# Three blocks of a transformer on one core: the rounded parts of the weights in a ring of four, split in the middle of a chunk

## What is computed

```
def _attention_layer(...):
    h = _rmsnorm(x, pre_g) * (1 + scale) + shift
    proj = h @ w_in                       # q, k, v, z
    outA = _dense_attention(...); outB = _window_attention(...)
    y = jnp.concatenate([outA, outB], axis=-1) * jax.nn.silu(z)
    x = x + gate * _rmsnorm(y @ w_out, post_g)

def _pool_layer(...):
    proj = h @ w_in
    y = _multiscale_pool(...) * jax.nn.silu(proj[..., POOL_WIDTH:])
    x = x + gate * _rmsnorm(y @ w_out, post_g)

def second_block(...):
    proj = h @ w_in[layer]
    q_sb, k_sb, v_sb, z_sb, q_r, k_r, v_r, z_r = jnp.split(proj, split_at, axis=-1)
    oa = stick_breaking_attention(...) * silu(z_sb)
    qr = rotary(q_r); kr = rotary(k_r) * HEAD_DIM ** -0.5
    ob = head_group_norm(chunkwise_retention(qr, kr, vr), gain) * silu(z_r)
    x = x + gate * (jnp.concatenate([oa, ob], axis=-1) @ w_out[layer])
```

## Time and profile before

| | us |
|---|---|
| median of three runs | 2598.04 |
| the three runs | 2602.52, 2598.04, 2596.53 |
| the profiled execution | 2595.46 |
| its span | 2593.6 |

### The profile page before, as it was taken

How to read it: one execution, slowest core, us unless ns; L and a number is a source line. 1 busy time by engine, 2 the same in 40 slices (tenths; PEclk the granted TensorE clock), 3 DMA queues, 4 the chain that set the end, 5 groups by cost and what they waited for, 6 DMA issues and landing times.

```text
span 2593.6 us, 29840 instructions
## 1 busy us (share of the span) xinstructions
PE 2528.2 (97%) x11859; PEld 2027.7 (78%) x11859; DVE 1617.3 (62%) x2424; ACT 958.3 (37%) x1529; POOL 105.1 (4%) x115
## 2 busy tenths in 40 slices
PE   7999999999999999999999998999999999999998
PEld 4789777777777877888888887887788777787786
DVE  4456666677776758677776757356466477656432
ACT  4222434434454333332334333355455423233321
POOL 0000000000000103000000102000000000000000
PEclk8999999999999989999999998999999999999999
DMA  9945433444425745666645654323222255532342
GB/s 349 340 163 187 125 111 114 122 124 133 133 90 169 241 150 171 195 203 207 207 146 194 239 176 141 93 79 90 74 87 83 77 164 160 172 93 82 122 146 73
DMA packets 292877, 390.58 MB, mean 151 GB/s; under 512 B 11698, under 2 KB 221234, under 8 KB 288898
## 3 DMA queue, kind: packets, MB, share of 16 engines
q1 hardware_dynamic: 286608, 354.79, 43.0%
q0 software_dynamic: 6128, 33.89, 3.4%
q10 hardware_dynamic: 2, 0.00, 0.0%
HBM read 371.85 MB, written 16.78 MB: 150 GB/s over the span
## 4 chain that ended last, share of the span: by engine, by line
PE 91%; DVE 4%; DMA 2%; ACT 1%; issue 1%; SPq 1%; POOL 0%; ACTq 0%; POOLq 0%; DVEq 0%
PE G L1962 77%; PE S L1962 6%; PE OB L1962 5%; PE TB L1965 2%; PE TB L1962 1%; DMA MORE<-in_ev_mod_w 1%; DMA MRAW<-in_ev_mod_w 1%; DVE Y L1473 1%; DVE TT L1473 1%; SPq L1019 0%; PE OB L1965 0%; DVE WLO L1473 0%; DMA LATE<-in_ev_mod_w 0%; DVE HLO L1479 0%; DVE SQ L1479 0%
## 5 line engine op out<-in xcount | busy, mean ns | idle before, releaser
L1962 PE MATMUL G<-HHI,WHI 128*128 128x512 f32 x2624 | 1088.9, 415 | 28.5 <-issue 7.7
L1962 PE MATMUL G<-HHI,WLO 128*128 128x512 f32 x2624 | 1031.2, 393 | 0.0
L1962 PE MATMUL G<-HLO,WHI 128*128 128x512 f32 x2624 | 1028.3, 392 | 0.0
L1473 DVE TENSOR_TENSOR WLO<-RAW,WHI 128x1024 fp32r<-128x1024 f32 x376 | 459.2, 1222 | 282.5 <-ACT WHI L1139 279.4
L1139 ACT ACTIVATE WHI<-RAW 128x1024 fp32r<-128x1024 f32 x376 | 394.8, 1054 | 583.1 <-PE G L1962 543.7
L1962 PEld LDWEIGHTS G<-HHI,WHI 128*128 128x128 f32 x2624 | 497.2, 189 | 139.2 <-issue 23.5
L1962 PEld LDWEIGHTS G<-HHI,WLO 128*128 128x128 f32 x2624 | 495.9, 189 | 108.4
L1962 PEld LDWEIGHTS G<-HLO,WHI 128*128 128x128 f32 x2624 | 498.0, 190 | 104.8 <-issue 8.1
L1479 DVE SCALAR_TENSOR_TENSOR MACC<-MWIDE,SC,MACC 128x512 f32<-128x512 f32 x420 | 321.3, 765 | 39.5 <-DMA MWIDE<-in_od_mod_w 13.5
L1962 PE MATMUL G<-WHI,HHI 128*128 128x512 f32 (+1 forms) x384 | 145.0, 378 | 3.9 <-ACT K L1139 3.0
L1962 PE MATMUL G<-WLO,HHI 128*128 128x512 f32 (+1 forms) x384 | 136.4, 355 | 0.0
(11 more groups left out here) (274 smaller groups left out, 2346.8 us busy)
## 6 DMA issues: line engine op xcount, KB each, us to landing
RAW<-in_w_in SPq DMA_DIRECT2D x128, 512.0 KB, 3.7
MWIDE<-in_od_mod_w SPq DMA_DIRECT2D x96, 512.0 KB, 4.2
MWIDE<-in_w_ada SPq DMA_DIRECT2D x96, 512.0 KB, 4.5
RAW<-in_ev_w_in SPq DMA_DIRECT2D x80, 512.0 KB, 3.8
RAW<-in_od_w_in SPq DMA_DIRECT2D x64, 512.0 KB, 3.9
MWIDE<-in_ev_mod_w SPq DMA_DIRECT2D x32, 512.0 KB, 3.9
RAW<-in_ev_w_out SPq DMA_DIRECT2D x32, 512.0 KB, 3.6
RAW<-in_od_w_out SPq DMA_DIRECT2D x32, 512.0 KB, 3.5
```

Source lines behind the costliest of these rows:

```text
L1473: return e.o.tensor_tensor(o, a, b, op)
L1962: return e.o.matmul(o, l, r, start=start, stop=stop, skip_group_check=True)
```

## The change

`NS` becomes 4. The ring WHI gets a fourth place, for the chunks with i % 4 = 3; the three others keep their tiles. The fourth lies over TA[0] and TA[1] (`WHI_TA`) as long as no stick-breaking head runs, and over Y[14] and Y[15] (`WHI_Y`) from chunk 232 to 299, while they do. Where a place changes its owner there are added waits: ACT's cast of the first chunk in Y waits for the spill of layer 3's input and its last tile, that of the next chunk in TA for the last stick-breaking sums, the first use of TA for chunk 231 (`last_ta`), and the last two rows of Y in layer 3 for chunk 299 (`last_y`).

The split moves from the end of a chunk to its middle (`split_ahead`), in `gemm_dual` behind the first pair of a chunk's matmul groups, ahead of `next(tiles)`. There it is that of chunk i + 3.

```
-    NR, NS = 5, 3
+    NR, NS = 5, 4
...
-    WHI = [place(f"WHI{i}", [P, 4, 256], F32R)[0] for i in range(NS)]
+    WHI3 = [place(f"WHI{i}", [P, 4, 256], F32R)[0] for i in range(3)]
...
+    WHI_TA = scratch("WHITA", [P, 4, 256], F32R, 46 * K1)
+    WHI_Y, _ = place("WHIY", [P, 4, 256], F32R, y0 + 4 * SEQ * 14)
...
+    stick0, stick1 = first_chunk[third + 2], first_chunk[third + 16] + 4
+    fourths = range(3, len(chunks), 4)
+    last_ta = max(i for i in fourths if i < stick0)
+    first_y = min(i for i in fourths if i >= stick0)
+    last_y = max(i for i in fourths if i < stick1)
+    next_ta = min(i for i in fourths if i >= stick1)
+
+    def whi(i):
+
+        if i % 4 < 3:
+            return WHI3[i % 4]
+        return WHI_Y if stick0 <= i < stick1 else WHI_TA
...
+        def split_ahead(i):
+            while at["split"] < min(i + NS, len(chunks)):
+                split_next()
...
@@ unit
-                while at["split"] < min(i + NS, len(chunks)):
-                    split_next()
...
@@ gemm (gemm_two, gemm_tok and gemm_wide alike)
                         put("mm", kind, layer, u, i, c, nt, jj, pair, last)
+                        if nt == 0 and jj:
+                            split_ahead(i)
                         step(background)
...
@@ gemm_dual
                     for nt in range(2):
                         put("mm2", "h", layer, u, i, c % 2, c // 2 * 4, nt, jj, (first + c) % 2)
+                    if jj == 0:
+                        split_ahead(i)
                     next(tiles, None)
                 used(i)
-                while at["split"] < min(i + NS, len(chunks)):
-                    split_next()
...
@@ act_program, stage "split"
+                if i == first_y:
+                    e.wait_ge(spill, 3)
+                    e.wait_ge(v_tile, (3, KT - 1))
+                elif i == next_ta:
+                    e.wait_ge(p_cum, (7, 0))
+                    e.wait_ge(v_st, (7, 0, "ls"))
+                    e.wait_ge(v_st, (7, 0, "lo"))
-                cp(WHI[i % NS][:, :, :], RAW[i % NR][:, :, :]).then_inc(*a_whi.up(i))
+                cp(whi(i)[:, :, :], RAW[i % NR][:, :, :]).then_inc(*a_whi.up(i))
...
@@ act_program, the first use of TA by a head
-                if (h, kt) != (0, 3):
+                if (h, kt) == (0, 3):
+                    e.wait_ge(p_gemm, last_ta)
+                else:
...
@@ dve_program, silu of layer 3
+                if layer == 3 and k >= 14:
+                    e.wait_ge(p_gemm, last_y)
```

More of the change, by code:

```diff
@@ L272, in build @@
     units += out_units(T["od_w_out"][0])
+    third = len(units)
     for p in range(4):
@@ L457, in work @@
                     put("mt", layer, u, i, c, t, pair, last, t == tiles - 1)
+                    if t == tiles // 2 - 1:
+                        split_ahead(i)
                     step(background)
@@ L469, in work @@
                     put("mw", layer, u, i, c, t, (first + t // 2) % 2, last, t == 3)
+                    if t == 1:
+                        split_ahead(i)
                     step(background)
@@ L1578, in dve_program @@
                 e.wait_ge(a_whi, i)
-                tt(WLO[i % NR][:, :, :], RAW[i % NR][:, :, :], f(WHI[i % NS][:, :, :]), SUB).then_inc(*v_wlo.up(i))
+                tt(WLO[i % NR][:, :, :], RAW[i % NR][:, :, :], f(whi(i)[:, :, :]), SUB).then_inc(*v_wlo.up(i))
             elif stage == "mod_acc":
@@ L2032, in pe_program @@
                 i = k // 4 * 2 + (0 if what == "k" else 1)
-                wh, wl, j = WHI[i % NS], WLO[i % NR], k % 4
+                wh, wl, j = whi(i), WLO[i % NR], k % 4
                 hi, lo = HHI[:, k, :], HLO[:, k, :]
@@ L2062, in pe_program @@
                 kind, layer, u, i, c, nt, jj, pair, last = a
-                wh, wl = WHI[i % NS], WLO[i % NR]
+                wh, wl = whi(i), WLO[i % NR]
                 cols = slice(nt * P, nt * P + P)
@@ L2125, in pe_program @@
                 layer, u, i, c, t_, pair, last, final = a
-                wh, wl = shaped(WHI[i % NS], 2), shaped(WLO[i % NR], 2)
+                wh, wl = shaped(whi(i), 2), shaped(WLO[i % NR], 2)
                 o, cols = G[pair][t_ % 2][:, :], slice(t_ * P, t_ * P + P)
```

## The result

The changed kernel takes 2607.76 us (median of six runs, 2604.47 to 2609.71), the kernel before 2599.73 (six runs, the three of above among them). The ratio is 1.0027, with a 95% interval of 1.0014 to 1.0039: slower by some 7 us. The forecast was 2597.0, in a range of 2590 to 2603. The profiled execution has a span of 2607.9 us, 14.3 more than that of before; it is the slowest of its six, and that of before (2595.46 us) is faster than all six of before, so the two traces differ by more than the medians.

The account below looks back on a forecast made before the run. PE was taken to bound the kernel, so only its waits count. Terms -1.7 - 1.8 - 1.9 + 0.7 + 0.3 + 3.4 = -1.0 us on the median 2598.04 gave 2597.0 us, range 2590 to 2603.

Parts of the forecast that it names:

- Part 1: WHI's fourth place and 1.5 chunks more lead: no more work for ACT or DVE, owner-change waits and earlier RAW cost 0.
- Part 6: Attention heads: moved casts and WLO delay some softmax exponentials and give back as much elsewhere; 0, ends -1 and +4.6 us.
- Part 2: The two short waits for WLO, chunks 317 and 322 in layer 3's retention heads, go: -1.7 us.
- Part 3: ACT's casts no longer stand ahead of three copies PE waits for: -1.8 us for KTA, -1.9 for two K copies.
- Part 4: Two DVE-bound stretches of layer 3's retention heads: WLO waits move to MACC and K; net +0.7 and +0.3 us.
- Part 5: The two layer changes, chunks 112 and 216: the split ahead of the tiles delays Y<-TB,Y by 1.7 us each, +3.4.
- The first rival: The deeper ring takes the waits in both DVE-bound stretches away in full: -15.7 us, 2582.3 us; chance 0.10.
- The second rival: Low clock paid in full in both stretches and at the layer changes: 10.4 us slower, 2607.4 us; chance 0.10.
- The third rival: DVE's WLO ahead of a windowed head's block maximum at four chunks delays a softmax: 4.6 us more, 2601.6; chance 0.06.
- The fourth: Rival: RAW lands late behind a MWIDE load, parts 2 to 4 give nothing, only +3.4: 2601.4 us; chance 0.04.

Follow-up runs that it names:

- shift64: The changed kernel with its fourth place 64 bytes further on (224256), two chunks using Y instead, one added ACT wait; 2609.52 us, ratio 1.0035.
- hi192: The changed kernel with its fourth place 192 bytes further on (224384), otherwise edited as shift64; 2601.16 us, ratio 1.0006.
- lo64: low_ta with the fourth place 64 bytes further on (161984), otherwise edited as shift64; 2609.35 us, ratio 1.0034.
- low_ta: The changed kernel, order untouched, with the work space below the weights' tiles, so the place over TA is at 161920; 2599.31 us, ratio 0.9998.
- mid3: The changed kernel's splits in the middle of a chunk, but a ring of three, two chunks ahead, no place over TA; 2600.30 us, ratio 0.9999.
- all64: The kernel before with its tiles 64 bytes further on, the work space only 32; 2602.19 us, ratio 1.0010.
- dual_low: low_ta with the split in `gemm_dual` back behind the tiles, at the end of the chunk; 2595.76 us, ratio 0.9981.
- khead: dual_low with the scores of a retention head waiting only for that head's own keys; 2591.84 us, ratio 0.9953.
- turnlate: khead with the second head's rotary 8 steps later, behind the first head's scores, for pairs up to head 13; 2587.96 us, ratio 0.9945.
- high3: The kernel before with the ring's three places at the top of memory (217024 to 229311), work space 12 KB lower; 2629.58 us, ratio 1.0117.

## Why the prediction was wrong, point by point

- **Part 1, the fourth place, was the step that failed.** "The number of casts and subtractions stays ... neither engine does more": I costed the ring's new place at nothing for ACT and DVE and never asked what PE, which reads it 24 times a chunk, pays. It pays 0.15 us a chunk in layer 2 (3.38 us) and 6.8 us in all. shift64 and hi192 differ in nothing but the start, and the ratios 1.0035 and 1.0006 are 7.5 us apart. Of the other pairs, hi192 has 1.06 us of PE's wait for Q that the changed kernel hasn't, and is still 5.5 us faster (1.0027 and 1.0006), and lo64, with the same wait, is 9.4 us slower than low_ta (1.0034 and 0.9998). The difference of 7 us to before lies between them. The layout could be computed from the code, and the trace of before has the price in it: where PHI, which begins 192 over a multiple of 256, is streamed past the weights, the steps are 0.2291 us (47 of them in 10.77 us), where they are 0.2274 in HHI's chunks of layer 2. So the place should have had a term with two bounds, as an operation has. The waits at the change of owner cost 0, as said. RAW's earlier load cost PE nothing either, but it isn't free of waits: ACT's casts wait 31.4 us in all for RAW, 8.0 at most, where it was 4.9 before.
- **The rest of the sum, -1.0 us,** agrees with the times, in part by luck. low_ta is the change without the slow place: 0.9998 (0.9989 to 1.0008, so -3 to +2 us), where -1.0 us is 0.9996. mid3 says the same for the moved splits. But the 4 us of part 6 below weren't in the sum; with them it would be +3, just past the end of that interval.
- **Part 2** (-1.7): held; no wait for WLO is left.
- **Part 3** (-1.8 and -1.9): held. The wait for KTA is gone, K copies wait for 1.2 us together where the earlier trace rows has 3.0.
- **Part 4**: the mechanism held. The wait moved to MACC, 5.24 us where 5.4 was forecast, and to K, 5.96 where 6.1 was. In the first stretch the net is +0.8 (forecast +0.7): the half clock lasts to 2193.6, 4.2 us of it with PE at work. In the second it is +1.6 (forecast +0.3): here the clock fell 4.7 us after PE had stopped, not 2.1, so 5.6 us of work lie in it instead of 2.9. I had taken the delay from one stall and used it as a constant. Such nets also move with the trace: all64, with the order of before, waits 1.2 us for MACC and 1.9 for K, where the earlier trace rows has 0.29 and 0.88.
- **Part 5** (+3.4): held. Y<-TB,Y starts 5.57 us later than in the earlier trace rows, MOD 4.05 later, so 1.5 us are new; dual_low takes them out again.
- **Part 6** (0, ends -1 and +4.6): missed, inside its ends. PE now waits 0.93 us for a softmax in layer 1 (PB at 769.29), and 0.77, 0.76 and 0.66 us for K in the stick-breaking heads, where ACT's cast now stands between the square and the root of the norm. With what follows each, that is some 4 us. mid3 has the same four waits, so they come with the moved splits. I had looked at one tight place only.
- **The first rival** (waits vanish in full) didn't come, for the reason argued: 5.2 and 6.0 us stand in their place. By the Trainium skill, Perfetto Trace Analysis, section Optimization Strategy, a gap that repeats on the engine that should be saturated can mean too few buffers, and the waits for WLO could be read so. The runs speak against that here: mid3 has one place fewer, no wait for WLO, and the same waits for MACC and K (5.4 and 6.1), and khead and turnlate remove or shorten those two with no more buffers.
- **The second rival** (low clock paid in full) took a part, some 1.7 us of its 10.4 in the two stretches.
- **The third rival** (a softmax delayed by WLO) came in one place, the 0.93 us of part 6, where DVE's WLO at 766.02 stands ahead of the block's maximum at 767.49. **The fourth** (RAW late, parts 2 to 4 give nothing) didn't come: ACT waits for RAW, PE for none of it.

In the profiled pair, the parts 2 to 5 sum to about 0, part 6 to some 4, and 1.7 more are a lower clock behind its wait in layer 1. The start-up is about 1.5 us longer: PE waits there for the loads of t_sq and of the modulation's weights, 0.8 and 1.1 us longer than before, for a reason that stays open. About 7 us are the growth without waits. Together these are the 14.3 us of the two spans.

## What to carry to other kernels

A new place for an operand is a change for the engine that reads it: compute where it starts relative to the tiles that stand in for it and to what is streamed beside it, and if steps of 0.2277 us become 0.2334 in one residue of the ring, look there first. A lag that grows in stretches without a wait can't be found in the list of waits; measure a dense stretch between two fixed instructions in both traces. And when a buffer is added for an engine that has no idle time, its wait comes back under the name of the next thing that this engine makes: shorten the chain, as turnlate did, or let fewer things wait for its end, as khead did.

## What the runs showed of the hardware

- Matmuls in fp32r whose weights begin at another offset within 256 bytes than the streamed tile and the other weights take 0.11 to 0.15 us more for 24 of them. Offsets of 192 and 0 against 128 are slow, 384 and 128 fast, at 158 KB as at 219 KB; moving all of them together changes little (layer 2 in 496.26 us against 495.47, and 505.36 in high3). The duration of a weight load in the rows is the same, 188 ns.
- The relation to the streamed tile is enough by itself: where high and low parts both begin at 128 and the streamed PHI at 192, 48 matmuls take 10.77 us, with all at 128 10.65, with the weights at 192 and PHI at 224 10.97. Which of the reads collide isn't shown. Nor is the reason why the attention chunks of layer 1 don't pay.
- Three of three places with the offset (high3) cost 0.11 us a chunk, one of three or four 0.15. I don't know why.
- The same stall doesn't always bring the clock down. PE waits 3.0 us for HLO near 784 us in dual_low and in khead. The windows of 10 us over it, of dual_low and of khead:

```profile
784.00:794.00 10.00, 9.37 (x32) 7.42 (x33) 3.69 (x8) 2.84 (x7) 0.00 (x0) 0.67 0.06 16
```

```profile
784.00:794.00 10.00, 10.00 (x51) 8.23 (x50) 4.38 (x8) 3.66 (x8) 0.00 (x0) 1.00 0.18 54
```

A clock of 0.67 and one of 1.00, after the same wait. 25 runs of the kernel before (those beside high3) lie between 2596.08 and 2607.66 us, with mean clocks of 0.979 to 0.984, the lower clock mostly with the longer time. So a difference of 2 or 3 us between two single traces says little.
